# A second block's mLSTM outputs computed with the score blocks as stationary operand, denominators as columns, and one transposition a head

## What is computed

```
scores = einsum('bhtd,bhsd->bhts', qc, kc) * d_mat
num = einsum('bhts,bhse->bhte', scores, vc) + w_inter[..., None] * einsum('bhtd,bhde->bhte', qc, c_st)
den = jnp.sum(scores, axis=-1) + w_inter * einsum('bhtd,bhd->bht', qc, n_st)
h_out = num / jnp.maximum(jnp.abs(den), jnp.exp(-m_t))[..., None]
...
h_m = mlstm_scan(forward) + flip_seq(mlstm_scan(backward))
mlstm_out = head_rmsnorm(h_m, mlstm_g, MLSTM_HEADS) * sigmoid(m_o)
return jnp.concatenate([hgrn_out, mlstm_out], axis=-1) @ w_out
```

## Time and profile before

| | us |
|---|---|
| median of 3 runs | 1701.24 (1700.75 to 1703.26) |
| span of the profiled execution, first to last instruction | 1698.8 |
| TensorE busy in it | 1648.8 (97%) |
| VectorE / ScalarE / GpSimd busy | 975.2 / 692.2 / 134.2 |
| the mLSTM stage, first `g` product to first `out2` product | 1061.0 to 1120.3 |

### The profile page before, as it was taken

The page is one execution under the profiler, slowest core; times in us unless marked ns, Lnnn a source line. Parts: engine busy times, 40 slices in busy tenths (PEclk is TensorE's granted clock), DMA queues, the critical chain, the costliest instruction groups (busy, mean ns, idle before and its releaser), DMA issues.

```text
span 1698.8 us, 18804 instructions
## 1 busy us (share of the span) xinstructions
PE 1648.8 (97%) x7210; PEld 1270.2 (75%) x7210; DVE 975.2 (57%) x1351; ACT 692.2 (41%) x1038; POOL 134.2 (8%) x144
## 2 busy tenths in 40 slices
PE   5999999999999999999999999999999999999997
PEld 1587765568788888887888787568877888888885
DVE  6957687674544324445888596665535463536352
ACT  4521465313533213335654668845434321212131
POOL 0211000142100000003000000222000100000001
PEclk9999999999999999999999999999999999999999
DMA  9534114313332243213142022325211222222221
GB/s 313 184 124 149 62 53 158 124 50 100 101 99 87 74 137 96 83 63 130 61 161 100 22 66 73 129 96 207 76 50 50 99 100 99 100 99 99 99 99 50
DMA packets 113560, 175.07 MB, mean 103 GB/s; under 512 B 3979, under 2 KB 56779, under 8 KB 112972
## 3 DMA queue, kind: packets, MB, share of 16 engines
q1 hardware_dynamic: 109724, 161.33, 28.0%
q0 software_dynamic: 3760, 12.72, 2.3%
HBM read 169.58 MB, written 4.46 MB: 102 GB/s over the span
## 4 chain that ended last, share of the span: by engine, by line
PE 82%; DVE 9%; ACT 4%; DMA 2%; issue 2%; SPq 1%; DVEq 0%; ACTq 0%
PE bank L880 16%; PE bank L882 16%; PE bank L881 16%; PE bank L917 6%; PE bank L918 6%; PE bank L922 5%; PE bank L1180 2%; DMA weight_slots<-in_w_mod 2%; PE bank L1195 2%; PE bank L1119 1%; PE bank L1131 1%; DVE weight_slots_lo L2349 1%; PE bank L1325 1%; PE bank L1410 1%; DVE arena L2885 1%
## 5 line engine op out<-in xcount | busy, mean ns | idle before, releaser
L3216 POOL TENSOR_TENSOR arena<-arena 128x512 f32<-128x512 f32 (+1 forms) x50 | 69.0, 1386 | 955.4 <-ACT arena L1627 952.5
L882 PE MATMUL bank<-hx_hi,weight_slots_lo 128*128 128x512 f32 x320 | 124.8, 390 | 0.0
L3171 DVE TENSOR_TENSOR weight_slots_lo<-weight_slots,weights_hi 128x2048 fp32r<-128x2048 f32 x30 | 67.4, 2289 | 97.7 <-ACT weights_hi L2308 97.7
L2308 ACT ACTIVATE weights_hi<-weight_slots 128x2048 fp32r<-128x2048 f32 x30 | 55.8, 1909 | 162.9 <-DMA weight_slots<-in_w_up 115.8
L1596 ACT ACTIVATE weights_hi<-weight_slots 128x2048 fp32r<-128x2048 f32 (+2 forms) x46 | 77.2, 1723 | 93.8 <-DMA weight_slots<-in_ffn_w_down 57.2
L881 PE MATMUL bank<-xn_lo,weights_hi 128*128 128x512 f32 x288 | 112.1, 389 | 0.0
L880 PE MATMUL bank<-sq_hi,weights_hi 128*128 128x512 f32 x256 | 99.6, 389 | 0.0
L881 PE MATMUL bank<-sq_lo,weights_hi 128*128 128x512 f32 x256 | 99.6, 389 | 0.0
L882 PE MATMUL bank<-sq_hi,weight_slots_lo 128*128 128x512 f32 x256 | 99.6, 389 | 0.0
L1582 ACT ACTIVATE arena<-bank 128x512 f32<-128x512 f32 (+2 forms) x107 | 53.2, 537 | 103.8 <-PE bank L882 50.4
L2349 DVE TENSOR_TENSOR weight_slots_lo<-weight_slots,weights_hi 128x2048 fp32r<-128x2048 f32 (+2 forms) x36 | 71.5, 2020 | 27.4 <-ACT weights_hi L1596 27.4
(11 more groups left out here) (441 smaller groups left out, 4078.2 us busy)
## 6 DMA issues: line engine op xcount, KB each, us to landing
weight_slots<-in_w_in SPq DMA_DIRECT2D x24, 1024.0 KB, 7.3
weight_slots<-in_ffn_w_up SPq DMA_DIRECT2D x22, 1024.0 KB, 6.5
weight_slots<-in_w_up SPq DMA_DIRECT2D x16, 1024.0 KB, 6.6
weight_slots<-in_w_down SPq DMA_DIRECT2D x16, 1024.0 KB, 6.2
weight_slots<-in_w_mod SPq DMA_DIRECT2D x14, 1024.0 KB, 10.1
arena<-in_w_mod POOLq DMA_DIRECT2D x32, 256.0 KB, 3.2
weight_slots<-in_w_out SPq DMA_DIRECT2D x8, 1024.0 KB, 7.4
weight_slots<-in_w_xkv SPq DMA_DIRECT2D x8, 1024.0 KB, 7.6
```

The costliest lines, as they stand in the source:

```text
L882: return mm(ps, ll, rh, start=False, stop=stop)
L2308: A(W_hi[:, s % 2, a:b], W[:, s % 2, a:b], ACT.Copy).then_inc(w_hi, 1)
L3171: V.tensor_tensor(W_lo[:, s % 2, a:b], W[:, s % 2, a:b], W_hi[:, s % 2, a:b].bitcast(F32), ALU.subtract).then_inc(w_lo, 1)
L3216: G.tensor_tensor(acc, acc, sq[i % 2][:, 0:width], ALU.add).then_inc(sq_added, 1)
```

## The change

- In `state_output` the roles turn: the 128 x 128 blocks of S are stationary, and the values of a head stream with a column of ones behind them (`VW` = 129 columns). For a target tile i the sources j follow each other; a direction has 10 blocks (1 + 2 in its first bank, 3 + 4 in its second). Results have the tokens on the partitions, and column 128 is the denominator. `num` and `den` jobs become `num_h_c_0` and `num_h_c_1`.
- The limits come as columns: `gcol`, four transpositions ahead of `mo_3`, copied to `limits`; the broadcast rows and their transfers go. VectorE's `head_limit` works on two columns and uses a reciprocal.
- ScalarE copies the forward half with the inverse as scale (`forward_scaled`); VectorE multiplies the backward half and adds it in one operation per tile (`directions_added`); ScalarE sums the squares of the head by its accumulator (`head_factor`); VectorE scales the head (`head_scaled`); TensorE transposes it in four pieces (`head_transposed`, job `ht_h`) in place of the norm sum; VectorE multiplies by gain and gate (`lstm_out`).
- In `first_products` of `out2` the middle call moves from tile 4 to tile 7, with the low products of tiles 0 to 6 behind it.
- POOL makes the low half 0 of `out2` slab 0, and loads `memT` earlier. Both `out2` slabs are loaded one after the other.

The diff, shortened. Left out: the wider arena (16 words put in behind the first 78 tiles, so that `Vm` holds 129 columns a head), the writing of `Vm` with its ones column, the buffers of `limits`, and the list of norms.

```diff
                 j += [f"ho_{h}", f"ho_{h + 1}", f"norm_ho_{h}", f"norm_ho_{h + 1}"]
     for h in range(-1, HEADS):
         if h >= 0:
-            j += [f"num_{h}_f", f"den_{h}_f"]
+            j += [f"num_{h}_f_{p}" for p in range(2)]
         if h + 1 < HEADS:
             j += [f"g_{h + 1}_{t}" for t in range(NT)]
         if h >= 1:
-            j += [f"norm_mo_{h - 1}"]
+            j += [f"ht_{h - 1}"]
         if h >= 0:
-            j += [f"num_{h}_b", f"den_{h}_b"]
-    j += [f"norm_mo_{HEADS - 1}"]
...
     done(sp, "mo_3")
     slab("out2", 0, io["w_out_2"], 0)
-    for h in range(1, HEADS):
-        for d in range(2):
-            evicted(sp, f"den_{h - 1}_{'fb'[d]}")
-            row(bg_rows[d], 1, 32 * d + h, f"ld_bg{d}")
-        if h == 1:
-            slab("out2", 1, io["w_out_2"], 512)
+    slab("out2", 1, io["w_out_2"], 512)
...
+        pe.wait_ge(sem("gate_g"), 1)
+        ps = begin("gcol")
+        for t in range(NT):
+            ins = nc.tensor.transpose(ps[:, 64 * t:64 * t + 64], m_g[0:64, P * t:P * t + P], ident[0:64, 0:64])
+        end(ins)
...
     def state_output(h, d):
         c = "fb"[d]
-        order = range(NT) if d == 0 else range(NT - 1, -1, -1)
-        for kind in ("num", "den"):
-            ps = begin(f"{kind}_{h}_{c}")
-            for n, j in enumerate(order):
-                if d == 0:
-                    pe.wait_ge(sem("S_ready"), NT * h + n + 1)
-                else:
-                    evicted(pe, f"g_{h}_{j}")
-                lo, hi = (P * j, L) if d == 0 else (0, P * j + P)
-                lhs = Vm[:, j, P * h:P * h + P] if kind == "num" else ones[:]
-                ins = mm(ps[:, lo:hi], lhs, S2[d][:, j, lo:hi], start=n == 0, stop=n == NT - 1)
+        for p, pair in enumerate(TILE_PAIRS[d]):
+            ps = begin(f"num_{h}_{c}_{p}")
+            for i in pair:
+                sources = range(i + 1) if d == 0 else range(NT - 1, i - 1, -1)
+                out_ = ps[:, VW * (i % 2):VW * (i % 2) + VW]
+                for j in sources:
+                    if d == 0:
+                        pe.wait_ge(sem("S_ready"), NT * h + j + 1)
+                    else:
+                        evicted(pe, f"g_{h}_{j}")
+                    ins = mm(out_, S2[d][:, j, P * i:P * i + P], Vm[:, j, h, :], start=j == sources[0], stop=j == sources[-1])
             end(ins)
+    def head_transposed(h):
+        pe.wait_ge(sem("mh_ready"), h + 1)
+        ps = begin(f"ht_{h}")
+        for i in range(NT):
+            ins = nc.tensor.transpose(ps[:, P * i:P * i + P], m_h[h % 2][:, P * i:P * i + P], ident)
+        end(ins)
     for h in range(-1, HEADS):
...
-            norm_sum(f"norm_mo_{h - 1}")
+            head_transposed(h - 1)
         if h >= 0:
             state_output(h, 1)
-    first_products("out2", "mix2", (mix2_hi, mix2_lo), middle=lambda: norm_sum(f"norm_mo_{HEADS - 1}"), at=4)
+    first_products("out2", "mix2", (mix2_hi, mix2_lo), middle=lambda: head_transposed(HEADS - 1), at=KD - 1, lows=KD - 1)
     w = split_slab("out2", 1)
...
+    def forward_scaled(h):
+        if h >= 2:
+            done(act, f"ht_{h - 2}")
+        for p, pair in enumerate(TILE_PAIRS[0]):
+            ps = full(act, f"num_{h}_f_{p}")
+            act.wait_ge(sem("den_inverse"), 2 * h + p + 1)
+            for i in pair:
+                ins = A(m_h[h % 2][:, P * i:P * i + P], ps[:, VW * (i % 2):VW * (i % 2) + P], ACT.Copy, scale=stat[:, h % 2, i:i + 1])
+            free(ins, f"num_{h}_f_{p}")
+    def head_factor(h):
+        for p in range(2):
+            evicted(act, f"num_{h}_b_{p}")
+        st = stat[:, h % 2, :]
+        for i in range(NT):
+            ins = A(m_t[:, P * i:P * i + P], m_h[h % 2][:, P * i:P * i + P], ACT.Square, accum_out=st[:, 8 + i:9 + i])
+        ins.then_inc(sem("mo_squared"), 1)
+        act.wait_ge(sem("mo_squared"), h + 1)
+        A(st[:, 8:12], st[:, 8:12], ACT.Ln, scale=1.0 / P, bias=eps[:]).then_inc(sem("mo_log"), 1)
+        act.wait_ge(sem("mo_log"), h + 1)
+        A(st[:, 12:16], st[:, 8:12], ACT.Exp, scale=-0.5).then_inc(sem("mo_factor"), 1)
...
-        act.wait_ge(normed, sum(norms[f"norm_mo_{h}"]))
+        evicted(act, f"ht_{h}")
         split_x(mix2_hi[:, HC + h, :], mix2[:, HC + h, :])
     for h in range(HEADS):
-        if h == 1:
-            inverse_limit(0, 1)
-            head_squares(0)
+        forward_scaled(h)
         if h + 1 < HEADS:
             decay(h + 1, 1, "b")
-        else:
-            split_w("out2", 0, (1,))
-        if h >= 2:
-            inverse_limit(h - 1, 1)
-            lstm_high(h - 2)
-            head_squares(h - 1)
-        inverse_limit(h, 0)
         if h == 0:
             act.wait_ge(sem("ho_gated"), HEADS)
             for k in range(HC):
                 split_x(mix2_hi[:, k, :], mix2[:, k, :])
         else:
-            norm_factor(f"norm_mo_{h - 1}", features=P)
+            lstm_high(h - 1)
         if h + 2 < HEADS:
             decay(h + 2, 0, "f")
         elif h + 2 == HEADS:
             split_w("out2", 0, (0,))
-    inverse_limit(HEADS - 1, 1)
-    lstm_high(HEADS - 2)
-    head_squares(HEADS - 1)
-    norm_factor(f"norm_mo_{HEADS - 1}", features=P)
+        head_factor(h)
+        if h + 2 == HEADS:
+            split_w("out2", 0, (1,))
     lstm_high(HEADS - 1)
     split_w("out2", 1)
...
-            done(dve, f"den_{h - 1}_{c}")
+            done(dve, f"num_{h - 1}_{c}_1")
...
+    def head_limit(h, d, p):
+        name = f"num_{h}_{'fb'[d]}_{p}"
+        ps = full(dve, name)
+        i0 = min(TILE_PAIRS[d][p])
+        den, inv = ps[:, P:2 * VW:VW], stat[:, h % 2, 4 * d + i0:4 * d + i0 + 2]
+        link(V.scalar_tensor_tensor(inv, den, -1.0, limits[:, i0:i0 + 2, 32 * d + h], ALU.mult, ALU.max))
+        link(V.tensor_tensor(inv, den, inv, ALU.max))
+        return V.reciprocal(inv, inv)
+    def forward_limits(h):
+        for p in range(2):
+            head_limit(h, 0, p).then_inc(sem("den_inverse"), 1)
+    def directions_added(h):
+        for p, pair in enumerate(TILE_PAIRS[1]):
+            link(head_limit(h, 1, p))
+            name = f"num_{h}_b_{p}"
+            ps = PS[jobs[name] % 8]
+            evicted(dve, f"num_{h}_f_{1 - p}")
+            for i in pair:
+                r_ = m_h[h % 2][:, P * i:P * i + P]
+                ins = V.scalar_tensor_tensor(r_, ps[:, VW * (i % 2):VW * (i % 2) + P], stat[:, h % 2, 4 + i:5 + i], r_, ALU.mult, ALU.add)
+            free(ins, name)
+    def head_scaled(h):
+        dve.wait_ge(sem("mo_factor"), h + 1)
+        r_ = m_h[h % 2].rearrange("p (i c) -> p i c", i=NT)
+        V.tensor_tensor(r_, r_, stat[:, h % 2, 12:16].unsqueeze(2).to_broadcast([P, NT, P]), ALU.mult).then_inc(sem("mh_ready"), 1)
     def lstm_out(h):
-        rstd_is(f"norm_mo_{h}")
-        r_ = m_h[h % 2]
-        link(V.scalar_tensor_tensor(r_, r_, pc("mlstm_norm_2", h), rstd[:], ALU.mult, ALU.mult))
+        ps = full(dve, f"ht_{h}")
         dve.wait_ge(sem("gate_ready"), HC + h + 1)
-        V.tensor_tensor(mix2[:, 4 + h, :], r_, mix2[:, 4 + h, :], ALU.mult).then_inc(normed, 1)
-        dve.wait_ge(normed, sum(norms[f"norm_mo_{h}"]))
...
+        g = mix2[:, HC + h, :]
+        free(V.scalar_tensor_tensor(g, ps[:], pc("mlstm_norm_2", h), g, ALU.mult, ALU.mult), f"ht_{h}")
...
+    ps = full(dve, "gcol")
+    free(V.tensor_copy(limits, ps[:, 0:64 * NT].rearrange("p (t r) -> p t r", r=64)), "gcol")
+    evicted(dve, "gcol")
     head_scores(0, 0, "f")
     for h in range(HEADS):
         head_scores(h, 1, "b")
             head_normed(3)
             head_gated(3)
         else:
-            head_limit(h - 1, 1)
-        if h >= 2:
-            lstm_out(h - 2)
+            head_scaled(h - 1)
+        forward_limits(h)
+        if h + 1 == HEADS:
+            split_w("out2", 0, (1,))
         if h:
-            directions_added(h - 1)
-        head_limit(h, 0)
-        if h >= 2:
-            lstm_low(h - 2)
+            lstm_out(h - 1)
         if h + 1 < HEADS:
             head_scores(h + 1, 0, "f")
-        else:
-            split_w("out2", 0, (0,))
-        head_sum(h, 0)
+        directions_added(h)
         if h == 0:
             for k in range(HC):
                 split_x("mix2", k, mix2_lo[:, k, :], mix2[:, k, :], mix2_hi[:, k, :])
-    split_w("out2", 0, (1,))
-    head_limit(HEADS - 1, 1)
-    lstm_out(HEADS - 2)
-    directions_added(HEADS - 1)
-    lstm_low(HEADS - 2)
+        else:
+            lstm_low(h - 1)
+    head_scaled(HEADS - 1)
     lstm_out(HEADS - 1)
     lstm_low(HEADS - 1)
...
                                 ALU.mult).then_inc(sem("D_masked"), 1)
-    done(pool, "norm_mo_3")
+    pool.wait_ge(sem("D_masked"), 8 * HEADS)
+    done(pool, "gcol")
     load(memT, io["memT"].rearrange("(k p) t -> p k t", p=P), "mem")
+    split_half("out2", 0, 0)
     add_squares("norm_mem", MEM)
     for name in ("norm_xa", "norm_mlp", "norm_fin"):
```

(17 more changed lines are left out.)

61 lines of the change are left out of this document (18 added, 43 removed).

## The result

| | before | after |
|---|---|---|
| median, us | 1701.24 (1700.75 to 1703.26, 5 runs) | 1710.02 (1707.75 to 1710.51, 5 runs) |
| ratio after / before | | 1.0043, 95% interval [1.0031, 1.0055] |
| the profiled execution: span, us | 1698.8 | 1708.4 (its time is 1710.23) |
| mean granted TensorE clock | 0.995 | 0.986 |
| first `g` to `out2_0`, us | 59.3 | 58.8 (1063.27 to 1122.11) |

The change makes the kernel 0.43% slower by the ratio, some 7.3 us (the two medians lie 8.8 us apart). I had forecast 1700.0, no change that can be measured, with a range up to 1704.2. The stage was to become 6.9 us shorter and became 0.5 us shorter. The seam lost what I had said. Behind it another 3.9 us went, where I had 1.4.

What follows compares the result with a forecast made beforehand. TensorE's queue was taken as the bound. Stage -10.8, three clock falls +3.9, seam +4.2, its fall +1.4 gave -1.3 on the 1698.8 us span: 1697.5, plus 2.4 carried over, 1700.0 us; range 1695.8 to 1704.2.

Steps and rivals of the forecast that it cites:

- The seam: Before `out2_4`: `out2_0` completes late, so low halves come late; 27.9 us against 23.7, +4.2, TensorE waiting 5.7 us.
- Matmuls, transposes, loads: TensorE in the stage: ten blocks 2.2 us, seven 1.55, four transposes 0.44, weight loads adding nothing visible.
- The stage at full clock: Score start to score start at 2.4 GHz: 10.9, 12.5, then 6.6 us to the output product; 10.8 us earlier.
- POOL's half: POOL's low half of `out2` slab 0 takes 4.92 us, ends about 1107.5, 2 us before needed: zero cost.
- The clock: Three longer TensorE waits in the stage each bring half clock, 1.3 us each: +3.9; bounds 0 and 1.8 each.
- The rival of a clock that stays down through the stage: All TensorE work on the stage's path doubled, 10.9 in place of 3.9: +5.7, 1706.9 us; chance 0.08.
- Its fall: Half clock behind the seam's wait before `out2_4`: one more fall, +1.4 us.
- The range: Whole kernel: 1695.8 to 1704.2 us around 1700.0, leaving a tenth on each side.
- the two slower rivals: Clock down through the stage (1706.9, chance 0.08); block loads adding their time on TensorE (1708.5, chance 0.09).
- the rival that loads show: Each block instruction pays its load, 0.24 instead of 0.11 us: +8.6 together, +7.3, 1708.5; chance 0.09.

Runs made afterwards that it cites:

- c2_fillall: Changed kernel with POOL's half on VectorE, slab 1's split ahead of the residual sum, 5, 4, 4 extra score products in TensorE's waits: 1693.30 us, ratio 0.9944.
- a3_fill: Changed kernel with 5, 4 and 7 extra score products, results unused, in TensorE's three waits of the mLSTM stage: 1703.06 us, ratio 1.0005.
- the two experiments: Changed kernel with POOL's low half made by VectorE instead (1704.59 us), or made by POOL in four 128x512 pieces (1706.33 us).
- a4_order: Changed kernel with VectorE's next forward and backward scores back to back, ahead of the transposed head and the sum of directions: 1705.26 us, ratio 1.0020.
- c1_best2: Changed kernel with a4_order's order, slab 1 split before residual, no POOL half, VectorE pieces in waits, slab 0 high halves one head earlier, six extra products: 1695.50 us.
- c4_before_seam: Kernel before, with only out2's middle call moved to tile 7 and the low products of tiles 0 to 6 behind it: 1710.09 us, ratio 1.0037.

## Why the prediction was wrong

By its own steps, against the profile after:

- **Matmuls, transposes, loads: right.** Ten blocks 2.2 us forecast, 2.23 measured; transposes 0.44 and 0.44. The rival that loads show is out.
- **The stage at full clock: right.** Forecast 10.9, 12.5 and 6.6 us from score start to score start. `c2_fillall`, at full clock, has 11.0, 12.7 and 7.6 (1.4 of it a wait for the low halves, which VectorE alone makes there); `a3_fill` has 6.4 for the last (1108.22 to 1114.60).
- **POOL's half: the step that failed.** The prediction put it at zero, since POOL would end 2 us before it is needed. It did end in time, at 1113.64 against 1122.11 for `out2_0` (it ended 6 us later than forecast, and what needs it came later still). But it cost VectorE 3.2 us on the path, and 3.2 to 4.2 us in all by the two experiments. I had asked only when POOL's result is needed, never what POOL takes from VectorE while it works. The forecast's own rows held a hint: VectorE's halves took 5.44 us for two at the seam against 2.28 each, and I had used it there alone.
- **The clock: mechanism right, term mis-sized.** Three falls at 1.3 us, +3.9, with 1.8 each as the bound. Measured 6.3 to 6.9, so 2.1 to 2.3 each, beyond the bound. The rows used showed a fall's cost where steady work follows. Here each is followed by the next wait, and 4.2 to 5.7 us of work ran at half speed, where the earlier trace rows have 3.4. The rival of a clock that stays down through the stage was partly true: the clock came back in each cycle, but late.
- **The seam: right in place and size.** Forecast 27.9 us and a wait of 5.7; measured 27.6 and 5.1. Its fall cost 2.1 instead of 1.4.
- **The range.** It ended at 1704.2, with a tenth left above it, although the two slower rivals (1706.9 and 1708.5) had a chance of 0.17 together. The price of the rival that loads show was also too low by its own rows: 512 columns take 0.43 us (3.43 for eight instructions), 129 take 0.11, so load and columns in turn are 0.30 us, not 0.24. It did not come true.
- **What lies outside.** A wait of 1.28 and 0.36 us near 1306 stands in the kernel before too, without a fall; in the profile after it has one (row 1307.00 above, 0.66), some 1.7 us. Ten of the fourteen profiles have it, those of before, a4_order, c1_best2 and c2_fillall don't. The first `g` comes 2.3 us later than in the profile before. The kernel c4_before_seam, the same as before up to there, has it at 1062.45, and the eleven experiments on the changed kernel, whose edits come later, lie between 1061.72 and 1064.40. So some 1.5 of the 2.3 us are no effect of the change, and the profiled execution of before was an early one. The granted clock shows about 1 us of it: behind the wait near 431 of the earlier trace rows it is 1.00 from 434.3 to 437.3 in the profile of before, and still 0.50 there in those of the change and of c4_before_seam.

On the spans: forecast -1.3, measured +9.6, a gap of 10.9. It is 2.3 for the first `g`, 3.2 for POOL's half, 3.2 left in the stage, which the falls nearly explain (2.4 to 3.0 over my 3.9 by a3_fill), -0.3 for the seam, and 2.5 behind it (0.7 of it the seam's fall, the rest the one near 1307). The ratio puts the loss at 7.3 us, so about 2 us of the spans' gap is chance of single profiles. What is open is why a wait of 1.6 us in all brings the clock down in one execution and not in another.
